# Dilated attention on one core: gate tiles one head later, output tiles started among the last head's rows, v projected with its weights stationary

## The reference, cut to what matters

```python
h = rms_norm(x, norm_g) * (1 + scale) + shift
k, v = jnp.split(h @ w_kv, 2, axis=-1)        # 6 k heads and 6 v heads of 128
...
qz = h @ w_in                                 # 24 q heads of 128, and the gate z of 8 x 128
q = rms_norm(q, q_norm_g) * (HEAD_DIM ** -0.5)
for g, (window, d) in enumerate(DILATED_GROUPS):   # dilation 1, 4, 16
    o, lse = dilated_group_attn(q[:, :, hs], kb, vb, slopes[hs], window, d)
...
o = jnp.sum(alpha[..., None] * jnp.stack(outs), axis=0)
y = o.reshape(bsz, s, B_WIDTH) * jax.nn.silu(z)
return x + gate * (y @ w_out)
```

## Time and profile before

| | |
|---|---|
| time, 3 runs | median 2104.47 us (2099.74 to 2106.39) |
| profiled execution | 2105.28 us, span 2103.6 us |
| PE busy | 1946.2 us, 93% of the span |
| DVE, ACT busy | 1130.7 us (54%), 777.8 us (37%) |
| granted TensorE clock, mean | 0.963 |
| v projection | 475.6 to 537.3 us |
| heads 0 to 7 with their tiles | 537.3 to 809.6 us |
| rows of the last head | 809.6 to 850.3 us |
| output projection | 850.3 to 893.9 us |
| up to the third feed-forward tile | 893.9 to 912.4 us |

### The profile page before, as it was taken

How to read it: one execution, slowest core, us unless ns; L and a number is a source line. 1 busy time by engine, 2 the same in 40 slices (tenths; PEclk the granted TensorE clock), 3 DMA queues, 4 the chain that set the end, 5 groups by cost and what they waited for, 6 DMA issues and landing times.

```text
span 2103.6 us, 23598 instructions
## 1 busy us (share of the span) xinstructions
PE 1946.2 (93%) x8692; PEld 1572.9 (75%) x8692; DVE 1130.7 (54%) x1548; ACT 777.8 (37%) x999; POOL 37.5 (2%) x96
## 2 busy tenths in 40 slices
PE   5999999989999996999999996999996979999997
PEld 4788888769888885778888873776654758888885
DVE  6346665475266655454434456598644464433445
ACT  3455553232255553332322233233334342232232
POOL 1000000000000000000000000000000000000000
PEclk8999999989999997999999998999998999999997
DMA  8445555412122221223233231232211213333321
GB/s 303 161 136 174 162 171 167 130 60 60 41 61 61 62 59 41 80 80 94 81 107 98 77 108 51 85 100 61 60 41 41 88 52 100 90 90 103 97 75 65
DMA packets 288195, 198.43 MB, mean 94 GB/s; under 512 B 6562, under 2 KB 275188, under 8 KB 287092
## 3 DMA queue, kind: packets, MB, share of 16 engines
q1 hardware_dynamic: 279568, 163.63, 27.0%
q0 software_dynamic: 8064, 33.56, 4.5%
q10 hardware_dynamic: 484, 0.16, 0.0%
HBM read 195.21 MB, written 2.11 MB: 94 GB/s over the span
## 4 chain that ended last, share of the span: by engine, by line
PE 84%; DVE 8%; ACT 3%; issue 3%; DMA 1%; DVEq 0%; POOL 0%; ACTq 0%; POOLq 0%
PE acc L573 19%; PE acc L575 19%; PE acc L574 19%; PE acc L777 3%; PE acc L779 3%; PE acc L778 3%; PE acc L1002 1%; DVE s_rstd L1509 1%; DMA s_ada_w<-in_a_ada_w 1%; PE ob L827 1%; PE acc L1004 1%; PE acc L1003 1%; PE acc L742 1%; ACT s_w_high L1060 1%; PE acc L744 1%
## 5 line engine op out<-in xcount | busy, mean ns | idle before, releaser
L1471 DVE TENSOR_TENSOR s_w_low<-s_raw,s_w_high 128x2048 fp32r<-128x2048 f32 x159 | 364.4, 2292 | 381.7 <-ACT s_w_high L1060 381.7
L573 PE MATMUL acc<-s_h_high,s_w_high 128*128 128x512 f32 x1248 | 493.5, 395 | 32.1 <-DVE s_h_low L1864 12.2
L574 PE MATMUL acc<-s_h_low,s_w_high 128*128 128x512 f32 x1248 | 487.3, 390 | 0.0
L575 PE MATMUL acc<-s_h_high,s_w_low 128*128 128x512 f32 x1248 | 487.2, 390 | 0.0
L1060 ACT ACTIVATE s_w_high<-s_raw 128x2048 fp32r<-128x2048 f32 x159 | 303.0, 1906 | 24.0 <-PE sc L658 18.0
L573 PEld LDWEIGHTS acc<-s_h_high,s_w_high 128*128 128x128 f32 x1248 | 235.3, 189 | 91.5 <-issue 35.2
L575 PEld LDWEIGHTS acc<-s_h_high,s_w_low 128*128 128x128 f32 x1248 | 235.2, 188 | 49.4
L574 PEld LDWEIGHTS acc<-s_h_low,s_w_high 128*128 128x128 f32 x1248 | 235.3, 189 | 48.5 <-issue 1.4
L573 PE MATMUL acc<-s_b_high,s_w_high 128*128 128x512 f32 x592 | 236.5, 399 | 27.7 <-DVE s_branch L2055 15.8
L574 PE MATMUL acc<-s_b_low,s_w_high 128*128 128x512 f32 x592 | 233.1, 394 | 0.0
L575 PE MATMUL acc<-s_b_high,s_w_low 128*128 128x512 f32 x592 | 232.7, 393 | 0.0
(11 more groups left out here) (293 smaller groups left out, 2368.8 us busy)
## 6 DMA issues: line engine op xcount, KB each, us to landing
s_raw<-in_a_w_in SPq DMA_DIRECT2D x48, 512.0 KB, 5.0
s_raw<-in_ffn_w_gate SPq DMA_DIRECT2D x44, 512.0 KB, 4.0
s_raw<-in_ffn_w_up SPq DMA_DIRECT2D x44, 512.0 KB, 5.2
s_raw<-in_w_in SPq DMA_DIRECT2D x36, 512.0 KB, 4.2
s_raw<-in_b_w_in SPq DMA_DIRECT2D x32, 512.0 KB, 5.2
s_ada_w<-in_b_ada_w POOLq DMA_DIRECT2D x24, 512.0 KB, 5.2
s_raw<-in_ffn_w_down SPq DMA_DIRECT2D x32, 384.0 KB, 4.0
s_raw<-in_ffn_w_down SPq DMA_DIRECT2D x32, 320.0 KB, 3.7
```

The source lines that it names most:

```text
L573: pe.matmul(acc[b][:, :], w_high[:, o:o + P], hi, start=(k == 0), stop=False, skip_group_check=grouped)
L574: pe.matmul(acc[b][:, :], w_high[:, o:o + P], lo, start=False, stop=False, skip_group_check=grouped)
L575: mm = pe.matmul(acc[b][:, :], w_low[:, o:o + P], hi, start=False, stop=(k == nk - 1), skip_group_check=grouped)
L1471: dve.tensor_tensor(w_low[:, w], raw[:, w], w_high[:, w].bitcast(F32), ALU.subtract).then_inc(w_ready, 1)
```

## The change

1. v is projected like k, with weights stationary (24 matmuls of 512 columns for a tile); ACT copies the tile to `v_raw`, PE turns it in four transposes, and DVE copies it to `v1`.
2. The tiles of phase qz have a new order, `QZ`. Head 0 has three slots with tiles; from head 1 on slot 3 makes the gate tile of the head before; slot 3 of head 7 is empty; the gates of heads 6 and 7 stand in slots 0 and 1 of head 8. Since the weight chunks hold two tiles of this list, `next_high` and `next_low` now come in the slots where the tile's number is even.
3. `output` writes a float tile `yf`, and each head's y is split as it comes (`y_part` on ACT in slot 1, `y_rest` on DVE in slot 2).
4. In slots 2 and 3 of head 8 PE makes output tiles 0 and 1 without their last step, then a part of tile 2; the last step of the three follows when head 7 is there.
5. The split of x for the feed-forward stands inside the loop over the output tiles.

The core of the diff:

```diff
 ROW_COUNTS = (sum(n for _, n in ROWS_A), sum(n for _, n in ROWS_B), CONV * CT)
 
 
+QZ = [(0, 0), (0, 1), (0, 2)]
+for _s in range(1, NQ):
+    QZ += [(_s, 0), (_s, 1), (_s, 2)] + ([(_s - 1, 3)] if _s < NQ - 1 else [])
+QZ += [(NQ - 2, 3), (NQ - 1, 3)]
+
+
+def slot_tile(s, n):
+
+    if s == NQ:
+        return QZ.index((NQ - 2 + n, 3)) if n < 2 else None
+    if n < 3:
+        return QZ.index((s, n))
+    return QZ.index((s - 1, 3)) if 0 < s < NQ - 1 else None
+
+
 def row_width(r):
 
     return min(2, TT - r) * P + 2 * (TT - r) * QUAD
...
             q0 = C0["qz"] // 2
-            with sp.Fori(0, 8) as i:
+            at_qz = [n * D + s * P for s, n in QZ]
+            for i in range(8):
                 for s in range(2):
-                    chunk_paired(i + q0, s, W["b_in"], i * P + 2 * s * D, W["b_in"], i * P + (2 * s + 1) * D)
+                    chunk_paired(i + q0, s, W["b_in"], at_qz[4 * i + 2 * s], W["b_in"], at_qz[4 * i + 2 * s + 1])
...
-            def v_tokens(g, b, s):
...
-                pe.wait_ge(evac[b], T0["kv"] // 2 + 3 + g)
-                for j in range(2):
-                    t = 2 * b + j
-                    for k in range(KD):
-                        o = s * SLOT + k * 2 * P
-                        hi, lo = tokens(b_high, k, t), tokens(b_low, k, t)
-                        to = acc[b][:, j * 2 * P:(j + 1) * 2 * P]
-                        pe.matmul(to, hi, w_high[:, o:o + 2 * P], start=(j == k == 0), stop=False, skip_group_check=True)
...
-            for m in range(3):
+                    for j in range(2):
+                        n = 2 * (m - 3) + j
+                        pe.wait_ge(evac[j], T0["kv"] // 2 + m + 1)
+                        if n >= 2:
+                            pe.wait_ge(v1_stored, n - 1)
+                        for t in range(TT):
+                            v_t = v_raw[j][:, t * P:(t + 1) * P] if n < NKV else \
+                                v_raw[j][:, :].rearrange("p (i t) -> p t i", t=4)[:, t, :]
+                            mm = pe.transpose(sc[1 + j][:, t * P:(t + 1) * P], v_t, ident[:, :])
+                        mm.then_inc(v1_turned, 1)
+
+            for m in range(6):
                 chunk(C0["kv"] + m)
                 product(0, T0["kv"] // 2 + m, m % 2, wide, 0, b_high, b_low, 0, KD,
                         *((h_ready, KD) if m == 0 else ()))
                 if m > 0:
                     kv_after(m - 1)
                 product(1, T0["kv"] // 2 + m, m % 2, wide, 1, b_high, b_low, 0, KD)
...
-            for m in range(3, 6):
-                chunk(C0["kv"] + m)
-                v_tokens(m - 3, 0, m % 2)
-                if m == 3:
-                    kv_after(2)
-                v_tokens(m - 3, 1, m % 2)
+            kv_after(5)
...
+            def tile_half(t, h):
+
+                b = t % 2
+                if b == h == 0:
+                    chunk(C0["qz"] + t // 2)
...
                         pe.wait_ge(h_ready, 2 * KD + k + 1)
-                    o = n // 2 * SLOT + paired(k, b)
+                    o = t // 2 % 2 * SLOT + paired(k, b)
...
-            for b in range(2):
-                pe.wait_ge(evac[b], T0["qz"] // 2)
+            pe.wait_ge(v1_stored, KVH)
...
+            bo_bank = [acc[0], acc[1], sc[1], sc[2], acc[0], acc[1], acc[0], acc[1]]
+
+            def bo_part(i, k0, k1):
+
+                if i % 2 == 0 and k0 == 0:
+                    chunk(BQ + i // 2)
+                if k0 == 0:
+                    if i < 2:
+                        pe.wait_ge(evac[i], BT)
+                    elif i < 4:
+                        pe.wait_ge(scores_taken, 4 * NQ)
+                    else:
+                        pe.wait_ge(evac[i % 2], BT + (1 if i < 6 else 3))
+                for k in range(k0, k1):
+                    if i < 3:
+                        pe.wait_ge(h_ready, 3 * KD + k + 1)
...
+                    hi, lo = y_high[:, k * T:(k + 1) * T], y_low[:, k * T:(k + 1) * T]
...
+                if k1 == KD:
+                    mm.then_inc(tile_ready, 1)
+
+            def project(s, n, h):
+
+                if slot_tile(s, n) is not None:
+                    tile_half(slot_tile(s, n), h)
+                elif s == NQ:
+                    bo_part(n - 2, 4 * h, 4 + 3 * h)
+
             for s in range(NQ + 1):
                 for n in range(4):
-                    if s < NQ:
-                        q_half(s, n, 0)
-                        if n == 3:
-                            square_sums(s)
+                    project(s, n, 0)
+                    if s < NQ and n == 3:
+                        square_sums(s)
                     if s > 1 and n == 1:
                         weighted(s - 2, (s - 2) // 4)
                     if s > 0:
                         scores(s - 1, (s - 1) % 2, (s - 1) // 4, n)
-                    if s < NQ:
-                        q_half(s, n, 1)
+                    project(s, n, 1)
                     if s > 0 and n > 0:
                         turn(s - 1, n - 1)
                     elif s > 1:
                         turn(s - 2, 3)
+            bo_part(2, 0, 4)
             turn(NQ - 1, 3)
             weighted(NQ - 1, 1, last=True)
+            bo_part(2, 4, KD - 1)
+            for i in range(3):
+                bo_part(i, KD - 1, KD)
+            for i in range(3, KD):
+                bo_part(i, 0, KD)
...
-                        v_g = v1[:, :].rearrange("p (k h d) -> p k (h d)", h=KVH, d=P)
-                        act.activation(v_g[:, 2 * t:2 * t + 2, (m - 3) * 2 * P:(m - 2) * 2 * P],
-                                       acc[t][:, :].rearrange("p (k e) -> p k e", e=2 * P), ACT.Copy).then_inc(evac[t], 1)
+                        n = 2 * (m - 3) + t
+                        if n >= 2:
+                            act.wait_ge(v1_turned, n - 1)
+                        act.activation(v_raw[t][:, :], acc[t][:, :], ACT.Copy).then_inc(evac[t], 1)
...
+            def y_part(a):
+
+                high_of(yf[a % 2][:, :], y_high, a, o_taken, a + 1, h_high_ready)
...
-                    if s < NQ:
-                        leave(s, n)
+                    if s > 1 and n == 1:
+                        y_part(s - 2)
+                    if t is not None:
+                        leave(t)
                     if s > 0 and n > 0:
                         store_g12(s - 1, n - 1)
                     elif s > 1:
                         store_g12(s - 2, 3)
-                    if s < NQ and n % 2 == 0:
-                        next_high(s + q0, n // 2, 4 * s + (t0 + n))
+                    if t is not None and t % 2 == 0:
+                        next_high(q0 + t // 4, t // 2 % 2, t0 + t)
+                    if s == NQ and n == 2:
+                        next_high(bo_q, 0, TILES_END["qz"])
...
-            for k in range(KD):
...
+            y_part(NQ - 1)
...
+            for i in range(KD):
+                if i > 0 and i % 2 == 0:
+                    next_high(bo_q + i // 4, i // 2 % 2, t0 + i)
+                act.wait_ge(evac[i % 2], t0 // 2 + i // 2 + 1)
+                high_of_x("ffn1_norm_pre_2", i)
+                square(xT[:, i * T:(i + 1) * T], i % 2, 2, i)
...
+                    for j in range(2):
+                        n = 2 * (m - 3) + j
+                        dve.wait_ge(v1_turned, n + 1)
+                        dve.tensor_copy(v1[:, :].rearrange("p (k h d) -> p k h d", h=KVH, d=P)[:, :, n, :],
+                                        sc[1 + j][:, :].rearrange("p (k d) -> p k d", d=P)).then_inc(v1_stored, 1)
...
+                z_at = QZ.index((a, 3))
+                dve.wait_ge(evac[z_at % 2], t0 // 2 + z_at // 2 + 1)
+                if a > 1:
+                    dve.wait_ge(h_high_ready, 3 * KD + a - 1)
+                    dve.wait_ge(h_ready, 3 * KD + a - 1)
                 dve.wait_ge(pv_ready, a + 1)
...
+            def y_rest(a):
+
+                low_of(yf[a % 2][:, :], y_high, y_low, a, h_high_ready, 3 * KD + a + 1, h_ready)
...
-                    if s < NQ and n % 2 == 0:
-                        next_low(s + q0, n // 2)
+                    if t is not None and t % 2 == 0:
+                        next_low(q0 + t // 4, t // 2 % 2)
+                    if s > 1 and n == 2:
+                        y_rest(s - 2)
+                    if s == NQ and n == 2:
+                        next_low(bo_q, 0)
...
+            for i in range(KD):
+                if i > 0 and i % 2 == 0:
+                    next_low(bo_q + i // 4, i // 2 % 2)
+                residual(t0 + i + 1, i % 2, i, GATE_B, bo_bank[i])
+                if i > 0:
+                    low_of_x("ffn1_norm_pre_2", 4, i - 1)
+                add_square(2, i, i % 2)
+            low_of_x("ffn1_norm_pre_2", 4, KD - 1)
```

105 lines of the change are left out of this document (50 added, 55 removed).

## The result

The changed kernel takes 2137.5 us (median of 4 runs, 2136.0 to 2139.6) against 2103.4 for the kernel before on the same chip. The ratio is 1.0157, 95% interval 1.0131 to 1.0182: slower by 34 us. The span of its profiled execution is 2134.3 us, 30.7 longer than before.

What follows compares the result with a forecast made beforehand. PE's pace bounded the heads, with a chain through DVE and ACT only a little shorter. Terms -19.5 + 40.4 - 4 - 5 + 9 = +20.9 us on 2105.3 gave 2126 us, slower by 1.0%, range 2106 to 2150.

Steps and rivals of the forecast that it cites:

- the clock in the heads: Heads: new waits cut PE's work into pieces, so some matmuls run at 1.2 GHz; +9 us.
- The clock falls in most heads: Rival, in the heads: slow clock costs +20 to +30 us, giving 2137 to 2147; chance 0.17.
- v: v projection: stationary weights give 144 contiguous 512-column matmuls instead of 288 short, partly strided ones; -19.5 us.
- The closed chain: Heads: chunk conversions behind rows 1 and 3 close a loop through ACT, DVE and PE, 42.7 us a head; +40.4 us.
- walk: Heads: step-by-step sum of one head in the new order, from PV to PV; 42.7 us, against 34.40 measured before.
- the walk with the old places: Heads: the same step sum with the weight chunk behind rows 0 and 2; 34.6 us, against 34.40 measured.
- the two pairs: Heads: two high-and-low-part conversions of a weight chunk per head, each counted as 4.21 us of the loop.
- both pieces that lengthen a head: Heads: PV with its scores, 3.8 us, and square sums, scores, half a tile, 5.8 us; both slow, about +5 a head.
- 1.4 a head: Heads: slow-clock loss taken for six and a half heads, since each wait but one is shorter than 3.4 us.
- The tail and the join: Last head's rows with output projection, -4 us; start of the feed-forward, with x's splits beside output tiles, -5 us.
- The other side: Rival on the faster side: heads stay at PE's pace and only the savings are left, 2077 us; chance 0.11.
- the rival in which the heads keep PE's pace: Heads: the chunk's two steps do not hold up the scaling, only savings of -28.5 us remain, 2077; chance 0.11.

Runs made afterwards that it cites:

- e2_v_alone: Kernel before with only the v projection changed to stationary weights, transposes and copies: 2086.1 us, ratio 0.991.
- e4_fill: Changed kernel with extra 128-column matmuls where PE waits in the heads (before transposes of rows 1 and 3, before PV): 2138.4 us, ratio 1.015.
- e3_before_chunk_odd: Kernel before with only the weight chunk's high and low part moved one slot earlier, behind rows 1 and 3: 2171.2 us, ratio 1.031.
- e1_chunk_even: Changed kernel with only the weight chunk's high and low part put back behind rows 0 and 2: 2085.5 us, ratio 0.989.
- e5_sums_split: Changed kernel with each head's square sums spread over slots 2 and 3, 8 one-column matmuls at a time instead of 24: 2117.5 us, ratio 1.004.
- e7_even_wide_sums: Changed kernel with chunks back behind rows 0 and 2, and each square sum 32 equal columns wide instead of one: 2073.8 us, ratio 0.984.
- e9_change_wide_sums: Changed kernel, chunks still behind rows 1 and 3, with each square sum 32 equal columns wide instead of one: 2131.8 us, ratio 1.012.
- e11_even_split_wide: Changed kernel with chunks back behind rows 0 and 2, square sums split over slots 2 and 3 and 32 columns wide: 2083.1 us, ratio 0.988.

## Why the prediction was right, and where its size was off

The forecast was 2126 us, slower; measured are 2137.5, inside the range of 2106 to 2150. Direction and mechanism are as forecast. The figure itself is 11 us off, nearly all of it in one term, the clock in the heads, and the outcome lies at the lower edge of the rival *The clock falls in most heads* (2137 to 2147, 0.17).

- **v:** -21.4 against -19.5. `e2_v_alone` gives 20.5 us alone. The larger part of the difference is the slow start: after a wait of 3.46 us PE's matmuls were slow for some 3 us and not for 6, which costs about 1.6 us (an estimate: eight matmuls in 3.38 us, against 0.227 each) instead of 3.0. The transposes and the end cost less than I took as well: the last ones are a group of 0.74 us and a wait of 0.78 for DVE's copy.

```profile
475.25:480.00 4.75, 4.75 (x14) 3.79 (x15) 4.22 (x4) 1.64 (x4) 0.00 (x0) 0.67 0.00 0
...
513.21 0.63 PE L756 MATMUL sc<-s_ident,s_v_raw 128*128 128x128 f32 x4
514.05 0.74 PE L756 MATMUL sc<-s_ident,s_v_raw 128*128 128x128 f32 x4 [0.22 <-ACT s_v_raw L1233]
515.58 0.50 PE L783 MATMUL acc<-s_h_high,s_w_high 128*128 128x512 f32 x1 [0.78 <-DVE s_v L1810]
```

  The Trainium skill (TensorE: Matmul & The Clock Gate, section LDWEIGHTS) lets a weight load depend on its columns alone, by which this term would have been near zero. The run disagrees, with 20.0 us less in the v projection. In the kernel before, the two durations both stand at a granted clock of 1.00 (0.19 us at 488, 0.33 at 501), so the slow clock is not what parts them.
- **The closed chain:** right in mechanism, places and length, apart from the clock. Step by step in the head at 679.69, the rows give 4.6 us from `output` to the exponential (walk 4.59), 4.2 for each pair of high and low part (4.21), 3.6 for tops of row 2 (3.63), 4.4 for tops of row 0 (4.41) and 2.1 from there to PV (2.13). The waits before row 1's transposes and before PV are 2.4 and 3.07 us, before those of row 3 1.1, and before the square sums of head 7 4.8 (forecast 2.6, 3.3, 1.4 and 4.7). Before the other square sums PE waits for 0.4 us and not for the 2.1 of the forecast, because it comes late itself, by slow matmuls at PV and at row 1's transposes; in `e4_fill`, without these, the wait is 2.0. `e3_before_chunk_odd` makes this chain without any other edit, `e1_chunk_even` opens it without undoing any other. One check in the prediction, that the walk with the old places gives 34.6, can't be redone from its steps: without the two pairs 34.3 are left, and 33.7 without the split of y.
- **The clock in the heads:** this is the term that was mis-sized, +9 against some +21. The prediction had both pieces that lengthen a head, PV and what follows the square sums, and its price with both slow, about +5 a head, is right: the two heads of 47.4 us are 4.7 above the walk. Its step that failed is how often: it took 1.4 a head, because each wait but one would be shorter than 3.4 us. The waits of 3.07 us before PV were enough in all six, and 1.4 a head is about what PV alone costs (the heads of 44.0 and 44.2 us are 1.3 and 1.5 above the walk). Behind the square sums the clock fell in four of the six stretches as well: 1.6 us in the head of 45.8, 3.2 in each of the heads of 47.4, and some 4 of the last stretch's 6.0, where it fell as PE waited 4.8 us for them. The prediction looked for the cause in PE's waits only. `e1_chunk_even` shows such a fall with no wait directly in front of it, and `e5_sums_split`, `e7_even_wide_sums` and `e9_change_wide_sums` speak for a part of the sums themselves in it, without settling its size.
- **The tail and the join:** -3.9 and -4.9 against -4 and -5. The output tiles' waits for y_low of head 6 and for the chunk of tile 4 were forecast at 3.4 and 2.3 us and are 3.26 and 2.18; the second is in this row:

```profile
908.83 0.50 PE L886 MATMUL acc<-s_y_high,s_w_high 128*128 128x512 f32 x1 [2.18 <-DVE s_w_low L1527]
```

- **The other side:** the rival in which the heads keep PE's pace was priced at 2077. It needed only the chunk in its old place: `e1_chunk_even` takes 2085.5, since the clock falls in four of its six stretches, and `e7_even_wide_sums`, the version with the lowest median, 2073.8, 32 us below the kernel before.

Open stays why the clock falls at the square sums in most heads of `e1_chunk_even` and in the kernel before only in the last two, where the same 24 matmuls stand in the same place, and which part of the 9.3 us between `e7_even_wide_sums` and `e11_even_split_wide` is the wait before PV.

## What to carry to other kernels

When a tile order is changed, look at what hangs on the parity of a tile's number: here the conversion of a weight chunk moved by one slot, in front of two steps that PE waits for, and that cost more than all the intended gains together. Walk one period through the in-order engines, step by step from start to start, and compare the length of that loop with the busiest engine's own work; busy shares of 53% and 36% said nothing. And look where TensorE runs many matmuls with hardly any columns: their own time is small, but in several heads here the matmuls behind them ran at half the clock.
